# Two transformer blocks on one core: high and low activations as one moving operand in four of seven block products

## The reference

```python
D_MODEL = 1024; SEQ = 512; D_FF = 2816        # D_FF_2 is 2816 too
...
        h = rms_norm(x, norm_ffn_pre[l])
        f = (jax.nn.silu(h @ w_ffn_gate[l]) * (h @ w_ffn_up[l])) @ w_ffn_down[l]
        x = x + rms_norm(f, norm_ffn_post[l])
...
        h = rms_norm_2(x, norm2_g[l])
        x = x + (jax.nn.silu(h @ w_gate[l]) * (h @ w_up[l])) @ w_down[l]
```

## Time and profile before

| | us |
|---|---|
| median of 3 runs | 1424.17 (1424.1 to 1424.84) |
| profiled execution, whole | 1423.1 |
| its span | 1421.0 |

### The profile page before, as it was taken

How to read it: one execution, slowest core, us unless ns; L and a number is a source line. 1 busy time by engine, 2 the same in 40 slices (tenths; PEclk the granted TensorE clock), 3 DMA queues, 4 the chain that set the end, 5 groups by cost and what they waited for, 6 DMA issues and landing times.

```text
span 1421.0 us, 22216 instructions
## 1 busy us (share of the span) xinstructions
PE 1408.6 (99%) x8248; PEld 1203.6 (85%) x8248; DVE 803.7 (57%) x1418; ACT 714.8 (50%) x1254; POOL 806.3 (57%) x470
## 2 busy tenths in 40 slices
PE   9999999999999999999999999999999999999999
PEld 6888888888788878999998887777677899999887
DVE  5426656775534257676753437889665676764000
ACT  5243434766753264666652226666665566664221
POOL 4434323762254479777754546766247887775443
PEclk9999999999999999999999999999999999999999
DMA  6433221211133334232334334322124332323433
GB/s 198 146 90 89 88 61 45 61 58 48 60 89 102 91 119 146 92 118 92 119 99 136 107 104 148 103 61 75 46 74 140 127 113 97 119 90 124 129 104 119
DMA packets 40339, 143.04 MB, mean 101 GB/s; under 512 B 4688, under 2 KB 4944, under 8 KB 39728
## 3 DMA queue, kind: packets, MB, share of 16 engines
q1 hardware_dynamic: 38976, 139.08, 31.4%
q10 hardware_dynamic: 1264, 2.62, 0.6%
HBM read 135.40 MB, written 6.29 MB: 100 GB/s over the span
## 4 chain that ended last, share of the span: by engine, by line
PE 90%; DVE 3%; POOL 3%; issue 2%; ACT 1%; DMA 0%; SPq 0%; DVEq 0%; POOLq 0%; ACTq 0%
PE bank L1619 12%; PE bank L1621 12%; PE bank L1620 11%; PE bank L1973 8%; PE bank L1975 8%; PE bank L1974 8%; PE bank L1648 3%; PE bank L1650 3%; PE bank L1649 3%; PE bank L2085 3%; PE bank L2086 2%; PE bank L2087 2%; PE bank L1867 1%; PE bank L1902 1%; PE bank L1887 1%
## 5 line engine op out<-in xcount | busy, mean ns | idle before, releaser
L680 POOL TENSOR_TENSOR wL<-raw,wH 128x1024 fp32r<-128x1024 f32 x165 | 405.9, 2460 | 482.9 <-ACT wH L871 350.5
L871 ACT ACTIVATE wH<-raw 128x1024 fp32r<-128x1024 f32 x136 | 143.8, 1057 | 313.1 <-PE bank L1621 250.0
L1619 PE MATMUL bank<-aH,wH 128*128 128x512 f32 x376 | 148.1, 394 | 0.2 <-POOL wL L680 0.2
L1620 PE MATMUL bank<-aL,wH 128*128 128x512 f32 x376 | 146.4, 389 | 0.0
L1621 PE MATMUL bank<-aH,wL 128*128 128x512 f32 x376 | 146.4, 389 | 0.0
L1619 PE MATMUL bank<-fH,wH 128*128 128x512 f32 x352 | 137.1, 390 | 0.0
L1620 PE MATMUL bank<-fL,wH 128*128 128x512 f32 x352 | 137.0, 389 | 0.0
L1621 PE MATMUL bank<-fH,wL 128*128 128x512 f32 x352 | 137.0, 389 | 0.0
L1973 PE MATMUL bank<-aH,wH 128*128 128x256 f32 x408 | 115.5, 283 | 1.0 <-POOL wL L762 1.0
L1975 PE MATMUL bank<-aH,wL 128*128 128x256 f32 x408 | 115.3, 282 | 0.0
L1974 PE MATMUL bank<-aL,wH 128*128 128x256 f32 x408 | 115.2, 282 | 0.0
(11 more groups left out here) (458 smaller groups left out, 3847.6 us busy)
## 6 DMA issues: line engine op xcount, KB each, us to landing
raw<-in_w SPq DMA_DIRECT2D x200, 512.0 KB, 3.5
raw_too<-in_w SPq DMA_DIRECT2D x34, 512.0 KB, 3.9
kept_x<-xT SPq DMA_DIRECT2D x4, 1024.0 KB, 6.1
xT<-kept_x SPq DMA_DIRECT2D x8, 512.0 KB, 5.0
bmk<-in_bias SPq DMA_DIRECT2D x6, 512.0 KB, 4.8
out_x<-xT SPq DMA_DIRECT2D x8, 256.0 KB, 4.4
xT<-in_x SPq DMA_DIRECT2D x3, 512.0 KB, 7.8
ct<-in_ct ACTq DMA_DIRECT2D x3, 384.0 KB, 3.5
```

What stands on the lines that cost most here:

```text
L680: pool.tensor_tensor(wL[:, c_slot, :], raw[:, c_slot, :], wH[:, c_slot, :].bitcast(F32), ALU.subtract).then_inc(sem("w_lo"), 1)
L871: act.activation(wH[:, s, :], raw[:, s, :], ACT.Copy).then_inc(sem("w_hi"), 1)
L1619: pe.matmul(bank[:], hi, H[:, ka, :], start=(k == 0), stop=False)
L1620: pe.matmul(bank[:], hi, L[:, ka, :], start=False, stop=False)
```

## The change

1. **PE, halves.** p2, p3, p4 and p5 use a new `product_in_halves`: a k-step has one matmul of 512 columns (high weights by H and L side by side, which lie in one tile `a_split` now) and one of 256 (low weights by H). The bank's left half then holds the high products, its right half the product with L, and the two have to be added. p1, p6 and p7 stay as they were.
2. **DVE, the additions.** c11, c12 and c22 become two instructions each. The first (`c11_part`, `c12_part`, `c22_part`) adds the bank's left half to the ACT copy, in place of the copy; the second waits for it and adds the bank's right half. u1 becomes the sum of the left half and a new ACT copy of the right half (`keep_low_side`); u2 scales all 512 columns, and waits for u1.
3. **The feature.** `gated_feature` writes the feature to SBUF (`f_full`, in the place of fL) instead of the PSUM bank, and `high_f` reads it there. Its low part is made by POOL (`feature_low`), no longer by DVE: for pair j-2 behind the low part of s4(j), and for the last two behind two chunks of the down product's weights.
4. **ACT.** `keep_low_side`(j-1) comes in behind the high part of s1(j). For pair 0, `keep_u3` is moved ahead of the high part of s2(1).
5. **PE, `mid`.** It runs behind the fourth k-step of the second plain tile, not ahead of that tile; it occurs in gu2 alone.

```diff
-                act.activation(fH[:, j, :], tmp[:, j % 2, :] if src is None else src[:], ACT.Copy).then_inc(sem("ff_fH"), 1)
+                act.activation(fH[:, j, :], tmp[:, j % 2, :] if src is None else src, ACT.Copy).then_inc(sem("ff_fH"), 1)
...
+            def keep_low_side(base, j):
+                if base + j:
+                    act.wait_ge(sem("pair_dve"), after("u1", base + j))
+                act.wait_ge(sem("pair_pe"), after("p4", base + j + 1))
+                act.activation(low_side, A_BANK[j % 2][:, right], ACT.Copy).then_inc(sem("pair_act"), 1)
...
                 high_s4(base, 0)
+                keep_u3(base, 0)
                 high_s2(base, 1)
                 for j in range(1, n):
-                    keep_u3(base, j - 1)
                     if j >= 2:
-                        high_f(p, first + j - 2, F_BANK)
+                        keep_u3(base, j - 1)
+                        high_f(p, first + j - 2, f_full[:, first + j - 2, :])
                     high_s3(base, j)
                     keep_p1(base, j)
                     high_x12(base, j)
                     if j < n - 1:
                         high_x11(base, j + 1)
                     high_s1(base, j)
+                    keep_low_side(base, j - 1)
                     high_x22(base, j)
...
+            def feature_low(p, j):
+                pool.wait_ge(sem("ff_fH"), KF * stage_of(p) + j + 1)
+                pool.tensor_tensor(fL[:, j, :], f_full[:, j, :], fH[:, j, :].bitcast(F32), ALU.subtract).then_inc(sem("ff_fL"), 1)
...
                     part_low("s4", s4_sum(j), base + j + 1)
+                    if j >= 2:
+                        feature_low(p, first + j - 2)
+                for c in range(2):
+                    low((dn.c0 + c) % 2, dn.c0 + c + 1)
+                for j in range(n - 2, n):
+                    feature_low(p, first + j)
...
-                    if mid is not None and t == (1 if p.name == "gu2" else 2):
-                        mid()
...
+                        if mid is not None and (t, k) == (1, 3):
+                            mid()
...
+                def product_in_halves(bank, part, act_, opens, closes):
+
+                    hi, lo = W_SPLIT[part]
+                    for k in range(KD // 2):
+                        at = slice(k * P, (k + 1) * P)
+                        pe.matmul(bank[:].rearrange("p (a s) -> p a s", a=2), hi[:, at], act_[:, :, k, :], start=opens and k == 0,
+                                  stop=closes and k == KD // 2 - 1, skip_group_check=True)
+                        mm = pe.matmul(bank[:, left], lo[:, at], act_[:, 0, k, :], start=False, stop=closes and k == KD // 2 - 1,
                                        skip_group_check=True)
                     mm.then_inc(sem("pair_pe"), 1)
...
-                    product(2, B_BANK, "x12", y21, True, True)
+                    product_in_halves(B_BANK, "x12", y21, True, True)
...
-                dve.wait_ge(sem("pair_dve"), after("u1", base + j + 1))
                 dve.wait_ge(sem("pair_dve"), after("u2", base + j + 1))
                 dve.wait_ge(sem("ff_silu"), feature(p, p.nt // 2 + j))
-                dve.tensor_tensor(F_BANK[:], F_BANK[:], sq[:, j % 2, :], ALU.mult).then_inc(sem("ff_f"), 1)
-                low_f(p, p.nt // 2 + j, F_BANK[:])
+                dve.tensor_tensor(f_full[:, p.nt // 2 + j, :], F_BANK[:], sq[:, j % 2, :], ALU.mult).then_inc(sem("ff_f"), 1)
...
-                dve.tensor_tensor(F_BANK[:, right], C_BANK[:, left], u3_copy, ALU.add).then_inc(sem("pair_dve"), 1)
+                dve.tensor_tensor(u3_copy, C_BANK[:, left], u3_copy, ALU.add).then_inc(sem("pair_dve"), 1)
+                dve.wait_ge(sem("pair_dve"), after("c22_part", base + j + 1))
+                dve.tensor_tensor(F_BANK[:, right], C_BANK[:, right], u3_copy, ALU.add).then_inc(sem("pair_dve"), 1)
...
-                dve.tensor_tensor(F_BANK[:, left], A_BANK[j % 2][:, left], nr[:, left], ALU.mult).then_inc(sem("pair_dve"), 1)
-                dve.wait_ge(sem("pair_dve"), after("c22", base + j + 1))
-                dve.tensor_tensor(F_BANK[:, right], F_BANK[:, right], nr[:, right], ALU.mult).then_inc(sem("pair_dve"), 1)
+                dve.wait_ge(sem("pair_act"), after("low_kept", base + j + 1))
+                dve.tensor_tensor(F_BANK[:, left], A_BANK[j % 2][:, left], low_side, ALU.add).then_inc(sem("pair_dve"), 1)
+                dve.wait_ge(sem("pair_dve"), after("u1", base + j + 1))
+                dve.tensor_tensor(F_BANK[:], F_BANK[:], nr[:], ALU.mult).then_inc(sem("pair_dve"), 1)
...
-                dve.tensor_tensor(G_BANK[:, left], B_BANK[:, left], p1_copy, ALU.add).then_inc(sem("pair_dve"), 1)
+                dve.tensor_tensor(p1_copy, B_BANK[:, left], p1_copy, ALU.add).then_inc(sem("pair_dve"), 1)
+                dve.wait_ge(sem("pair_dve"), after("c11_part", base + j + 1))
+                dve.tensor_tensor(G_BANK[:, left], B_BANK[:, right], p1_copy, ALU.add).then_inc(sem("pair_dve"), 1)
...
-                dve.tensor_tensor(G_BANK[:, right], C_BANK[:, left], u2_copy(j), ALU.add).then_inc(sem("pair_dve"), 1)
+                dve.tensor_tensor(u2_copy(j), C_BANK[:, left], u2_copy(j), ALU.add).then_inc(sem("pair_dve"), 1)
+                dve.wait_ge(sem("pair_dve"), after("c12_part", base + j + 1))
+                dve.tensor_tensor(G_BANK[:, right], C_BANK[:, right], u2_copy(j), ALU.add).then_inc(sem("pair_dve"), 1)
```

More of the change, by code:

```diff
@@ L271, in two_blocks_kernel @@
         wL = sb("wL", [P, 2, CW], F32R)
-        aH = sb("aH", [P, KD, S], F32R)
-        aL = sb("aL", [P, KD, S], F32R)
+        a_split = sb("a_split", [P, 2, KD, S], F32R)
+        aH, aL = a_split[:, 0], a_split[:, 1]
         sq = sb("sq", [P, 2, S])
@@ L353, in two_blocks_kernel @@
                 t_work = sb("t_work", [P, 4, KD // 2, HS], F32, over)
+            with ExitStack() as over:
+                f_full = sb("f_full", [P, KF, S], F32, over)
             fL = sb("fL", [P, KF, S], F32R, ffn)
@@ L804, in _ @@
             opening_chunk(p, 11)
-            pairs(p)
-            lows(PH["dn1"].c0, i2 + 2)
+            pairs(p, PH["dn1"])
+            lows(PH["dn1"].c0 + 2, i2 + 2)
             pool.wait_ge(sem("w_hi"), i2 + 3)
@@ L844, in _ @@
             t_low(p, 3, 2)
-            pairs(p)
-            lows(PH["dn2"].c0, NCHUNK)
+            pairs(p, PH["dn2"])
+            lows(PH["dn2"].c0 + 2, NCHUNK)
         @block.scalar
@@ L1963, in pairs @@
                 base, n = PAIRS_BEFORE[p.name], PAIRS[p.name]
-                y11, y21 = ((aH[:, y_rows(p, h), left], aL[:, y_rows(p, h), left]) for h in range(2))
-                t4, y22 = ((aH[:, y_rows(p, h), right], aL[:, y_rows(p, h), right]) for h in range(2))
-                t1, t2, t3 = ((T_SPLIT[i][:, 0], T_SPLIT[i][:, 1]) for i in (1, 2, 3))
-                def product(n, bank, part, act_, opens, closes):
-                    (hi, lo), (H, L) = W_SPLIT[part], act_
+                y11, y21 = (a_split[:, :, y_rows(p, h), left] for h in range(2))
@@ L1971, in product @@
+                t4, y22 = (a_split[:, :, y_rows(p, h), right] for h in range(2))
+                t1, t2, t3 = (T_SPLIT[i] for i in (1, 2, 3))
+                def product(bank, part, act_, opens, closes):
+                    hi, lo = W_SPLIT[part]
                     for k in range(KD // 2):
                         at = slice(k * P, (k + 1) * P)
-                        pe.matmul(bank[:, left], hi[:, at], H[:, k, :], start=opens and k == 0, stop=False, skip_group_check=True)
-                        pe.matmul(bank[:, left], hi[:, at], L[:, k, :], start=False, stop=False, skip_group_check=True)
@@ L1975, in product @@
-                        mm = pe.matmul(bank[:, left], lo[:, at], H[:, k, :], start=False, stop=closes and k == KD // 2 - 1,
+                        pe.matmul(bank[:, left], hi[:, at], act_[:, 0, k, :], start=opens and k == 0, stop=False, skip_group_check=True)
+                        pe.matmul(bank[:, left], hi[:, at], act_[:, 1, k, :], start=False, stop=False, skip_group_check=True)
+                        mm = pe.matmul(bank[:, left], lo[:, at], act_[:, 0, k, :], start=False, stop=closes and k == KD // 2 - 1,
+                                       skip_group_check=True)
@@ new lines, in product @@
+                    mm.then_inc(sem("pair_pe"), 1)
+                def product_in_halves(bank, part, act_, opens, closes):
+                    hi, lo = W_SPLIT[part]
+                    for k in range(KD // 2):
+                        at = slice(k * P, (k + 1) * P)
+                        pe.matmul(bank[:].rearrange("p (a s) -> p a s", a=2), hi[:, at], act_[:, :, k, :], start=opens and k == 0,
+                                  stop=closes and k == KD // 2 - 1, skip_group_check=True)
+                        mm = pe.matmul(bank[:, left], lo[:, at], act_[:, 0, k, :], start=False, stop=closes and k == KD // 2 - 1,
@@ L1982, in p1 @@
```

(12 more changed lines are left out.)

22 lines of the change are left out of this document (12 added, 10 removed).

## The result

Six runs of the changed kernel have a median of 1430.87 us (1429.57 to 1433.6), six of the kernel before 1424.26 (1423.74 to 1424.84). The ratio is 1.0047, with a 95% interval of 1.0037 to 1.0058: slower, by 6.6 us on the medians. The forecast was 1432.3, slower than before. The profiled execution of the changed kernel took 1431.29 with a span of 1429.5; the span of before was 1421.0.

What follows compares the result with a forecast made beforehand. The feature's cycle through DVE and ACT, 10.28 us a round, was to replace PE as the bound: 6.2 + 0.6 + 3.2 - 1.9 = +8.1 on 1423.1 gives 1431.2, 1432.3 on the median's footing; 8-in-10 range 1419 to 1440.

Steps and rivals of the forecast that it cites:

- The cycle: Feature on DVE, its high part on ACT, s1's high, then low part, next feature: from 8.94 to 10.28 us a round.
- dependent starts of 0.46: On DVE, an instruction waiting for the 256-column one just ahead starts 0.46 us after it, in place of 0.33.
- dependent starts are not free: Denies the rival that dependent starts on DVE are free: cycle 9.89 us, time 1421.3; chance 12%.
- PE was not the bound: Denies the rival that the cycle does not close and PE stays the bound in the pairs: 1415.3 us; chance 14%.
- the one in between: Rival: some DVE additions cost less, cycle 10.0 to 10.1 us, time about 1424 to 1426, no change; chance 6%.
- the costlier additions: Rival: DVE's additions cost more, cycle from 10.5 us on, time over 1438; chance 9%.
- the upper bound of a dependent start: 0.53 us on DVE, read from c12 to gate_normed, where two waits precede the second: cycle 10.49, time 1438.1.
- Rounds: From p6(2) to the last p6 in gu1 and gu2, 28 rounds cost 0.22 us more each: +6.2.
- Entry: Ahead of the first feature in each pair stage, DVE's added work makes p6 0.3 us later: +0.6 for both.
- End: PE waits 1.6 us ahead of p4 of the last pair in each stage: +3.2.
- mid: PE's 1.82 us wait for the sum of squares is covered by four more k-steps: -1.9, 0 as other bound.
- PE's own saving: In p2 to p5, halves save 0.0128 us a k-step, 0.205 a round: PE's round from 10.06 to 9.855.

Runs made afterwards that it cites:

- experiment 1: Changed kernel with ACT making the feature's high part later, behind the high part of s1 and the new copy: 1419.57 us.
- experiment 2: Changed kernel without the first parts of c11 and c12, DVE adding only the bank's left half there: 1419.58 us.
- experiment 9: Changed kernel with c12's first part between s1 and s2, and c11's first part ahead of the low part of s2: 1419.78 us.
- experiment 4: Kernel before with only mid moved, behind the fourth k-step of the second plain tile: 1421.74 us.
- run 16: Not a follow-up run: the words are part of the sentence that PE had run 16 products of only two columns each.
- experiment 6: On top of experiment 1, the last keep_u3 ahead of the high part of the down product's first weights on ACT: 1420.45 us.
- experiment 7: Changed kernel with DVE's additions reordered: c12's first part, low part of s2, c12, c11's first part, gate_normed, c11: 1449.46 us.
- experiment 10: Changed kernel with the late high part, the last keep_u3 first and the additions apart, all three together: 1419.24 us.
- experiment 3: Changed kernel with the feature's low part back on DVE, behind the gated feature, and taken out on POOL: 1438.31 us.
- experiment 5: On top of experiment 1, a_split's high and low parts of a k-step lie 2 KB apart in place of 16 KB: 1419.89 us.
- experiment 8: On top of experiment 1, plain products of 256 columns in p2 to p5 again, the left half read twice: 1423.05 us.

## Why the prediction was right

**The cycle** was the mechanism, and its length was forecast as measured: 10.28. The terms of it (dependent starts of 0.46, the wider u2, the feature's high part from SBUF) are each in the rows above, and experiments 1, 2 and 9 shorten it in three different places with the results that it foretells. The rivals fall: dependent starts are not free (experiment 9), PE was not the bound, and 10.28 is neither the 10.0 to 10.1 of the one in between nor the 10.5 of the costlier additions. What the upper bound of a dependent start rested on, two waits ahead of it, is not shown: in the code s2 has two as well, and it reads 0.73 behind an s1 listed with 0.69, as with one.

The Trainium skill (VectorE: DVE Perf Modes, section "The DRAIN you can't avoid") states, of a chain of copies, that a semaphore after each costs nothing extra. That does not carry over to these additions, where the next one waits for the semaphore: 0.44 to 0.46 with a dependent start here, 0.33 without.

**Rounds:** 133.63 us for 13 in gu1 and 154.30 for 15 in gu2, against 130.69 and 150.80: 2.9 + 3.5 = 6.4, forecast 6.2.

**Entry:** from the first pair product to p6(2), 21.13 in place of 20.73 in gu1 and 21.75 in place of 21.37 in gu2: 0.4 each, forecast 0.3.

**End:** from the last p6 to dn, 11.40 in place of 10.17 and 11.30 in place of 10.05: 1.2 a stage, forecast 1.6. The mechanism was as forecast, the size in part. The gap ahead of the last p4, in the rows of s4, the down product's weights, p5's last matmul, keep_u3 and p4 (as the earlier trace rows):

```profile
729.30 0.68 DVE L2856 TENSOR_TENSOR tmp<-raw,bank 128x512 f32<-128x512 f32 x1
...
733.76 1.06 ACT L1317 ACTIVATE wH<-raw 128x1024 fp32r<-128x1024 f32 x1 [1.50 <-DMA raw<-in_w]
733.77 0.28 PE L2008 MATMUL bank<-t_split,w_too 128*128 128x256 f32 x1
734.73 0.37 ACT L1304 ACTIVATE ssum<-bank 128x256 f32<-128x256 f32 x1
...
735.24 0.47 PE L2006 MATMUL bank<-a_split,wH 128*128 128x512 f32 x1 [1.18 <-ACT ssum L1304]
```

p4 starts 10.79 behind the last round's feature (724.45), forecast 10.81. PE would have been there at 9.44 and not at 9.23, in part since its products are longer than priced, so the wait is 1.35 (735.24 less 733.77, less 0.12), and 1.24 in gu2. The forecast took the wait of 1.6 for the whole difference. It left out what the five products in halves behind the last p6 save: by its own price 5 x 4 x 0.0128 = 0.26 a stage, so this term should have been 2.7 for both stages, and the sum 7.6 and not 8.1.

**mid:** forecast -1.9, measured -2.07 alone (experiment 4). In the changed kernel's profiled execution only 0.39 of it is left, since TensorE's clock fell to its lower level for some us in that stretch:

```profile
980.00:985.00 5.00, 5.00 (x20) 3.74 (x20) 3.97 (x10) 2.80 (x7) 1.83 (x2) 0.66 0.10 42
```

The last three columns are the granted clock, the DMA share and GB/s; a clock of 0.66 over 5 us is 3.4 us at 1.2 GHz in place of 2.4, and costs 1.7. Ahead of it PE had run 16 products of only two columns each (977.64 to 979.44). In the profiles of experiments 1, 2, 6, 7, 9 and 10 the clock fell behind the same products. In those of 3 and 5 it did not, and the stretch takes 379.14 and 379.15, so the whole gain is there; nor did it fall there in those of 4, 8 and the kernel before. Why it falls in one execution and not in another is open.

**What was mis-sized** is PE's own saving: 0.205 a round was forecast, 0.11 measured (experiment 8). So PE's own round is 9.94 and not 9.855, and it lost 0.33 at p6 and not 0.42. Three plain matmuls were priced rightly at 0.36, the wide one with its narrow neighbour not: by the starts, the pairs of p2, p3 and most of p4 take 0.353 and not 0.3465 (592.47 to 592.71 is 0.24, where a plain one of 512 columns takes 0.227). Whether that comes of the two widths in turn, or of a moving operand in two pieces at all, is open; it is not the distance of the pieces (experiment 5). The error did not show in the time because PE was not the bound.

**What was wrong in the working** and hidden in the sum: the prediction gave nothing for taking the feature's low part off DVE. In the rounds that is so, at the end of a stage it is not (experiment 3).

In all, the parts give 6.4 + 0.8 + 2.5 - 2.1 = +7.6, with forecasts of 6.2, 0.6, 3.2 and -1.9. The clock's 1.7 is not in this sum. The medians differ by 6.6, 1.0 less; the single runs of the changed kernel are spread over 4 us, so what makes up that rest can't be told.

## What to carry to other kernels

An engine that is busy for 99% of the time need not stay the bound when it gets less to do: look for cycles between the other engines in the orders, and read their own length from a place where the busy engine has not yet caught up, as the first round here. Such a cycle can be cut by moving one instruction that nobody on it needs yet: here the feature's high part on ACT was worth 11 us, as much as leaving two additions out. Additions that depend on one another, back to back, took a third longer from start to start here than with other work between them; before such work is moved, the wait of every moved instruction has to be looked up.

## What the runs showed of the hardware

A DVE instruction whose two inputs both lie in SBUF took 2.18 us beside a POOL instruction, and 0.69 without one (experiment 3); in the kernel before, the same subtraction in the pairs had one input in PSUM and took 0.69. The ten low parts of the plain tiles, with both inputs in SBUF too, have a median of 2.11 there. The Trainium skill states that DVE and GpSimd share a pair of SBUF ports, and that of a DVE instruction with two SBUF inputs and a GpSimd instruction that reads SBUF the one that starts first holds the pair, and the other is fully blocked (SBUF — State Buffer, section "SBUF: two separate sides"). The rows agree: POOL's instruction began first and ended at 739.64, and DVE's 0.55 later. So an engine here did wait for another without a semaphore between them, other than the opening of this text says. And the prediction's "Nothing in DVE's rows shows it slower beside POOL" overlooked those ten rows. Its additions did not get slower all the same. Each has one input in PSUM, as s4 has, which in the changed kernel took 0.68 (729.30) while POOL worked from 727.64 to 730.19.

After a wait, a matmul's successor starts later than usual: 0.19 from p6's first to its second in place of 0.12.
